# Hybrid decoder trunk: the gate projections of scan groups 1 to 3 as seven-product pairs ahead of the scan, and each scan interleaved with an output projection

## The reference

```python
def ssd_mixer(u, w_in, conv_w, conv_b, dt_bias, A_log, D, norm_w, w_out):
    proj = u @ w_in
    z = proj[..., :SSD_INNER]
    xbc = proj[..., SSD_INNER:SSD_INNER + SSD_CONV_DIM]
    ...
    xbc = jax.nn.silu(causal_depthwise_conv(xbc, conv_w, conv_b))
    ...
    y = ssd_chunked(xs, dt, A, Bm, Cm) + xs.astype(jnp.float32) * D.astype(jnp.float32)[:, None]
    y = y.reshape(b, s, SSD_INNER) * jax.nn.silu(z.astype(jnp.float32))
    yg = y.reshape(b, s, SSD_GROUPS, SSD_INNER // SSD_GROUPS)
    yg = yg * lax.rsqrt(jnp.mean(yg * yg, axis=-1, keepdims=True) + EPS)
    y = yg.reshape(b, s, SSD_INNER) * norm_w.astype(jnp.float32)
    return y.astype(u.dtype) @ w_out
```

## Time and profile before

| what | us |
|---|---|
| runs, median of 3 | 2283.34 (2282.04 to 2283.8) |
| profiled execution, its own time | 2282.14 |
| its span, first to last instruction | 2280.4 |
| PE busy in the span | 2258.5 |
| DVE busy | 1320.3 |
| POOL busy | 1320.6 |
| ACT busy | 1101.5 |

### The profile page before, as it was taken

How to read it: one execution, slowest core, us unless ns; L and a number is a source line. 1 busy time by engine, 2 the same in 40 slices (tenths; PEclk the granted TensorE clock), 3 DMA queues, 4 the chain that set the end, 5 groups by cost and what they waited for, 6 DMA issues and landing times.

```text
span 2280.4 us, 28960 instructions
## 1 busy us (share of the span) xinstructions
PE 2258.5 (99%) x10698; PEld 1845.5 (81%) x10698; DVE 1320.3 (58%) x1716; ACT 1101.5 (48%) x2016; POOL 1320.6 (58%) x950
## 2 busy tenths in 40 slices
PE   8999999999999999999999999999999999999998
PEld 6877888888888878888878888888888888888887
DVE  7357663333335798855568484747854343336777
ACT  4046544333333446655567474737643333334445
POOL 3224288777774664787734242334388777774654
PEclk9999999999999999999999999999999999999999
DMA  5100323323227855233263323232222323228744
GB/s 164 47 28 19 120 64 112 120 88 120 88 102 259 268 161 166 93 112 119 86 222 123 120 84 118 86 102 93 102 88 97 122 84 122 85 106 292 250 148 155
DMA packets 170807, 281.45 MB, mean 123 GB/s; under 512 B 19232, under 2 KB 104108, under 8 KB 168108
## 3 DMA queue, kind: packets, MB, share of 16 engines
q1 hardware_dynamic: 167084, 267.68, 34.9%
q10 hardware_dynamic: 3584, 11.93, 1.3%
HBM read 209.71 MB, written 69.86 MB: 123 GB/s over the span
## 4 chain that ended last, share of the span: by engine, by line
PE 92%; DVE 3%; POOL 2%; issue 1%; ACT 1%; DMA 1%; SPq 0%; ACTq 0%; DVEq 0%; POOLq 0%
PE ps L2212 44%; PE ps L1925 8%; PE ps L1927 8%; PE ps L1926 8%; PE ps L2302 5%; PE ps L2306 5%; PE ps L2298 5%; PE ps L2592 1%; PE ps L2582 1%; PE ps L2575 1%; PE ps L1948 1%; PE ps L2370 1%; POOL sq L1205 1%; PE ps L2135 1%; PE ps L2168 1%
## 5 line engine op out<-in xcount | busy, mean ns | idle before, releaser
L1051 POOL TENSOR_TENSOR s_lo<-s_val,s_hi 128x512 fp32r<-128x512 f32 x154 | 235.5, 1533 | 196.7 <-ACT s_hi L1575 196.0
L2862 DVE TENSOR_TENSOR xres<-ps,xres 128x512 f32<-128x512 f32 x132 | 90.5, 688 | 400.2 <-PE ps L2212 400.2
L947 POOL TENSOR_TENSOR w_lo<-w_raw,w_hi 128x1024 fp32r<-128x1024 f32 x50 | 119.3, 2387 | 270.6 <-ACT w_hi L1239 205.9
L972 POOL TENSOR_TENSOR p_lo<-p_val,p_hi 128x512 fp32r<-128x512 f32 x176 | 239.4, 1369 | 48.6 <-ACT p_hi L1380 37.5
L1380 ACT ACTIVATE p_hi<-p_val 128x512 fp32r<-128x512 f32 x176 | 111.0, 632 | 307.8 <-POOL p_val L998 307.8
L2212 PE MATMUL ps<-xn_hi,p_hi 128*128 128x512 f32 x704 | 189.0, 390 | 1.2 <-ACT xres L1483 1.2
L2212 PE MATMUL ps<-xn_lo,p_hi 128*128 128x512 f32 x704 | 188.2, 389 | 0.0
L2212 PE MATMUL ps<-xn_hi,p_lo 128*128 128x512 f32 x704 | 188.2, 389 | 0.0
L1575 ACT ACTIVATE s_hi<-s_val 128x512 fp32r<-128x512 f32 x154 | 97.0, 630 | 160.8 <-DMA d_val<-in_w_down 89.9
L1925 PE MATMUL ps<-xn_hi,w_hi 128*128 128x512 f32 x400 | 160.3, 401 | 0.0
L1926 PE MATMUL ps<-xn_lo,w_hi 128*128 128x512 f32 x400 | 156.0, 390 | 0.0
(11 more groups left out here) (361 smaller groups left out, 5570.3 us busy)
## 6 DMA issues: line engine op xcount, KB each, us to landing
s_val<-hidden SPq DMA_DIRECT2D x154, 256.0 KB, 2.9
hidden<-xres SPq DMA_DIRECT2D x20, 1792.0 KB, 6.5
wv_g<-in_w_gate SPq DMA_DIRECT2D x22, 1024.0 KB, 5.2
wv_u<-in_w_up SPq DMA_DIRECT2D x20, 1024.0 KB, 5.1
d_val<-in_w_down SPq DMA_DIRECT2D x70, 256.0 KB, 4.1
rows_v<-in_w_down SPq DMA_DIRECT2D x64, 256.0 KB, 3.8
mdec<-decay_sums SPq DMA_DIRECT2D x32, 512.0 KB, 4.2
xres<-parked_x SPq DMA_DIRECT2D x24, 512.0 KB, 6.0
```

The lines of the kernel that those rows point to most:

```text
L947: pool.tensor_tensor(w_lo[piece.slot][:, :], raw[piece.raw][:, :], f(w_hi[piece.slot][:, :]), ALU.subtract).then_inc(lo_done, 1)
L972: pool.tensor_tensor(p_lo[n][:, :, :], src, f(p_hi[n][:, :, :]), ALU.subtract).then_inc(p_lo_done, 1)
L1051: pool.tensor_tensor(s_lo[i][:, :], s_val[i][:, :], f(s_hi[i][:, :]), ALU.subtract)\
```

## The change

It has two halves. First, the gate columns of groups 1, 2 and 3 (six blocks of 256 columns) become blocks of the input stage: `NQ` goes from 6 to 9, and they are done with seven products each. ACT applies SiLU as it reads the finished row from PSUM; SP stores the row to a new DRAM tensor `z_rows` (12 rows of 512 KB) and loads it back in halves of 1 MB (`load_z`). Group 0's gates stay in its scan.

```diff
-        NQ = 6
+        NQ = 9
...
-        Q_BLOCKS = [(0, "x0"), (0, "x1")] + [(g, n) for g in range(1, G) for n in ("bc", "x0", "x1")]
+        Q_BLOCKS = ([(0, "x0"), (0, "x1")] + [(g, n) for g in range(1, G) for n in ("z0", "z1")]
+                    + [(g, n) for g in range(1, G) for n in ("bc", "x0", "x1")])
...
+                if is_z(i):
+                    sp.wait_ge(z_row_done, of_kind(i))
+                    sp.dma_start(z_rows[(g - 1) * BG + k - NCB], row_buffer(i)).then_inc(row_stored[i % 4], 16)
...
+            def load_z(g, half):
+                cols = slice(half * BANK, (half + 1) * BANK)
+                z_src = z_rows[(g - 1) * BG:g * BG].rearrange("r p s -> p r s")
+                sp.dma_start(zs_at, z_src[:, :, cols]).then_inc(z_loaded, 16)
...
+                if is_z(i):
+                    act.activation(row_buffer(i), flat(row_banks(i)), ACT.Silu).then_inc(z_row_done, 1)
+                    return
```

```diff
+        Z_ORDER = [(0, 0), (0, 1), (1, 0), (2, 0), (3, 0), (1, 1), (2, 1), (3, 1)]
+        Z_AFTER_CHUNK = [(5,), (6, 7), (8,), (9,), (10, 11), (12, 13), (14,), (15,)]
+        SILU_AFTER_CHUNK = {1: (0, 1), 3: (2, 3), 5: (4, 5), 7: (6,)}
...
+        def sums_after(g):
+            return {7: 0} if g == 0 else {3: 1, 6: 2} if g == 1 else {2: 2 * g - 1, 6: 2 * g}
...
+        PIECE_HI = [{0: 2, 1: 3, 3: 4, 4: 5, 5: 6, 6: 7}, {1: 0, 3: 1, 4: 2, 6: 3}, {0: 0, 2: 1, 4: 2, 6: 3}, {0: 0, 2: 1}]
...
+                if k:
+                    pe.wait_ge(cb_freed, k)
+                    pe.wait_ge(m_ready, 2 * k)
...
+                    if g == 0:
+                        for i in Z_AFTER_CHUNK[c]:
+                            z_half(i)
+                    else:
+                        for n in (2 * c, 2 * c + 1):
+                            out_part(g - 1, n, range(BG)).then_inc(out_full, 1)
+                    if c in sums_after(g):
+                        square_sums(sums_after(g)[c])
...
+            def between(g, c):
+
+                if g == 0:
+                    if c == 6:
+                        gated(0, 0)
+                    if c == 7:
+                        rests(0, 0, range(BG - 1))
+                    return
+                if c == 0:
+                    if g == 1:
+                        rest(0, 0, BG - 1)
+                    else:
+                        add_tile(g - 2, NT - 1)
+                        reciprocal_rms(2 * g - 2)
+                        gated(g - 1, 1)
+                elif (g, c) == (1, 1):
+                    reciprocal_rms(0)
+                elif (g, c) == (1, 5):
+                    reciprocal_rms(1)
+                elif g >= 2 and c == 4:
+                    reciprocal_rms(2 * g - 1)
+                if c:
+                    add_tile(g - 1, c - 1)
+                if (g, c) == (1, 1):
+                    gated(0, 1)
+                if c == 4:
+                    if g == 1:
+                        rests(0, 1)
+                    gated(g, 0)
+                if g >= 2 and c == 3:
+                    rests(g - 1, 1)
+                if c == 7:
+                    rests(g, 0)
...
-                        four = mdec[c % 2][:, 4 * hf:4 * hf + 4, :]
-                        dve.tensor_tensor(four, four, cbm[c % 2][:, :].unsqueeze(1).to_broadcast([P, 4, P]), ALU.mult)\
+                        dve.tensor_tensor(four, four, ps[:, CB, 0:P].unsqueeze(1).to_broadcast([P, 4, P]), ALU.mult)\
...
+                        dve.tensor_tensor(ps[:, YDIAG, :], ps[:, YDIAG, :], e2, ALU.add).then_inc(ydiag_summed, 1)
...
+                    if (g, c) == (1, 0):
+                        silu_z(ZU - 1)
+                        root(0)
+                    if (g, c) == (1, 2) or g >= 2 and c == 1:
+                        split(g - 1, 1)
+                    if (g, c) == (0, 6) or g and c == 5:
+                        split(g, 0)
+                    if c in PIECE_HI[g]:
+                        next_hi(g, PIECE_HI[g][c])
+                    if (g, c) == (1, 4):
+                        root(1)
+                    if g >= 2 and c == 3:
+                        root(2 * g - 1)
+                    if g and c == 7:
+                        root(2 * g)
```

803 lines of the change are left out of this document (467 added, 336 removed), and 3 rows, old and new, of the table LO_AHEAD.

## The result

The changed kernel takes **2294.51 us** (median of 5 runs, 2292.84 to 2295.47) against 2283.39 us for the kernel before (5 runs, 2282.04 to 2286.2): a ratio of 1.0045, 95% interval 1.0031 to 1.0060. It is 11.1 us slower. The forecast was 2276.5 us, a gain of 6.8 us, with a range of 2266 to 2289: the measured time has the other sign and lies outside the range.

The account below looks back on a forecast made before the run. PE's list of matmuls was taken as the bound. -16.3 - 1.6 + 4.6 + 1.6 + 2.9 + 2.0 = -6.8 us from the profiled 2282.1, median 1.2 higher: 2276.5 us, range 2266 to 2289.

Parts of the forecast that it names:

- Fewer matmuls, 16.3 us: Gate projection on PE, groups 1 to 3: 72 matmuls gone at 0.227 us each, 16.3 us less.
- Rival D: Longer input stage runs below PE's pace, rows passing through four buffers: 1 us per block, 2282.5 us; chance 0.06.
- The next term, 1.6 us: Ends of groups 0, 1 and 2: PE's three 0.52 us waits for POOL's sum of squares go, 1.6 us less.
- nothing too, as the loads are asked for a chunk and more ahead.: DMA: storing and reloading the 12 gate rows, 12 MB added to 281 MB, costs nothing.
- What the scan now hides: Scan: whether helpers' work fits each shortened chunk; a plain chunk fits with 2.2 us to spare on DVE.
- +4.6 us, group 0's chunk 7: Group 0's chunk 7: PE waits 4.6 us for `masked_decay`, late behind ACT's SiLU, squares, high parts and exponentials.
- +1.6 us at the border: Border of groups 0 and 1: ACT's SiLU, root and table loads cost 1.1 us for chunk 8, 0.5 for chunk 9.
- +2.9 us in group 1: Group 1: low parts and gatings share the fifth chunk on DVE, wait 2.7 us, with 0.2 more near chunk 2.
- +2.0 us in groups 2 and 3: Groups 2 and 3: DVE's low parts, then additions and gatings, cost waits of 0.3 and 0.7 us per group.
- rival C: Groups 1 to 3 DVE bound, gatings and low parts meeting POOL: 2297 us in full; chance 0.19.
- Rival E: DVE pays 0.04 us for each of 192 operations reading PSUM, half in waiting chunks: 2280.5 us; chance 0.05.
- Rival A: The forecast: saving real, 8 to 14 us given back, most in group 0 by ACT; 2271 to 2283 us; chance 0.47.

Follow-up runs that it names:

- Run 1: Changed kernel with SyncE asking for the fourth weight piece ahead of the gate and row loads in chunk 5 of groups 1 to 3: 2284.18 us.
- run 5: Changed kernel with group 0's weight pieces 4 and 5 asked for one chunk earlier: 2289.01 us.
- Run 11: Kernel before, with the masked product kept in PSUM and PE's wait for the mask moved to the chunk's start, nothing else: 2297.17 us.
- run 2: Changed kernel with the masked product of B and C back in SBUF and PE's early wait for the mask removed: 2281.07 us.
- run 6: Changed kernel with runs 1 and 2 together: 2275.99 us.
- run 3: Changed kernel with group 0's first-half squares and high parts behind chunk 7's exponentials on ACT, low parts in group 1's chunk 0: 2297.81 us.
- run 7: Run 3 with group 0's last weight piece also asked for ahead of group 1's rows: 2294.14 us.
- run 10: Changed kernel with runs 1, 2, 3, 5 and 7 together, three low parts moved a chunk earlier and the seventh SiLU moved beside the eighth: 2264.67 us.

## Why the prediction was wrong

**Fewer matmuls, 16.3 us.** Right. The input stage is gapless, and with the waits mended the kernel ends at 2264.67 us, where 2283.4 - 17.9 = 2265.5 was due. Rival D is out. The next term, 1.6 us, holds as well: the three square-sum waits are gone.

**"nothing too, as the loads are asked for a chunk and more ahead."** This step, the price of the added loads, failed first. I judged the DMA by its mean busy share (a third) and by the order in which the loads are asked for. I never asked what stands ahead of a weight piece in SyncE's queue, nor what stands behind its split on ACT, where the next exponentials do. Run 1 puts 10.3 us on the piece's place behind those loads in groups 1 to 3, run 5 puts 5.5 us on two pieces of group 0.

**"What the scan now hides", the chunk sums.** This is the second step that failed. I did let PE need the mask at the next chunk's start, but applied that only where I had added work to DVE. The mask ends at T + 7.02 in my own row, and the chunks that have one part of the gate projection (12 matmuls) on PE last 6.48 us: 0.5 us late by the new point already in the kernel before, without any addition. Group 0 has three such chunks. I summed chunks 6 to 9 there and took chunks 1 to 5 as free. Their waits came to 4.7 us, with 1.4 us of clock behind the longest (that one owes most of its length to a late piece: run 5 leaves 0.57 of its 3.36 us). Run 11 shows what the omission is worth by itself: 14.2 us. It and the late pieces overlap, as runs 1, 2 and 6 show (10.3, 13.4, together 18.5), since a late mask costs more the earlier PE asks for it.

**+4.6 us, group 0's chunk 7.** Measured 5.05 us of wait, ended by the mask, with the squares ahead of ACT's exponentials, as I had worked it out. So near a size is in part luck, for the cause was only half of it: the late weight piece behind the squares gave nearly the same wait alone (run 3, 4.70 us). The lost clock, 2.7 us, was not in the sum.

**+1.6 us at the border.** Too high: nothing in group 1's chunk 0 and 0.18 us in its chunk 1. PE had waited in chunk 7, which gave ACT and DVE time to catch up; when that wait went (run 7), one of 3.29 us stood at the border.

**+2.9 us in group 1.** The chunk with low parts and gatings gave 2.18 us against my 2.7, and chunk 2 gave 0.26 against 0.2. The 2.24 us in chunk 7 was unforeseen, and came from the piece.

**+2.0 us in groups 2 and 3.** Chunk 5 of group 2 gave 0.83 us against 0.7. Chunk 7 of group 2 gave 3.30 unforeseen, and group 3 gave nothing. In group 3 ACT splits no piece in the later chunks (`PIECE_HI` has chunks 0 and 2 only), so none stands ahead of chunk 7's exponentials, which fits. The period of group 2 came out as 81.2 us (1449.19 to 1530.38 on PE), which the list of signs gave to rival C; in run 10 it is 73.6 us, near the 74 worked out.

**Rival C** had nearly the right time, 2297, for a wrong reason. It had low parts and gatings on DVE lengthened by POOL. Few were: of 32 low parts the median fell from 1268 to under 750 ns, and the gatings kept theirs (680 and 686 ns) with a shorter longest one. The rows are the low parts of the first halves of groups 1 to 3 and the gatings of groups 1 to 3 in the changed kernel; shortest, median and longest in ns, beside the earlier trace rows:

```profile
L3554 DVE SCALAR_TENSOR_TENSOR y_lo_c<-rows_v,gconst,y_hi_c x12: 744/748/750, 1440.2 to 1598.0; 128x512 fp32r<-128x512 f32 x12
...
L3542 DVE TENSOR_TENSOR rows_v<-rows_v x24: 679/686/1790, 1409.6 to 1603.1; 128x512 f32<-128x512 f32 x24
```

**Rival E and the page's rule.** Neither the mask multiplication nor the y operation became longer by reading PSUM (1.28 against 1.29 us for two, 344 against 346 ns for one). The difference of fixed cost between SBUF and PSUM in the Trainium skill ("VectorE: DVE Perf Modes", the errata section) does not show in them.

**Rival A's words** do not fit its numbers: 8 to 14 us given back of 17.9 would be 2273 to 2279 us, and its range says 2271 to 2283. Neither holds the result; 29 us were given back.

The prediction did say which readings would refute its picture, a wait for DMA among them. It looked for that wait on PE, though, and it was two engines away, on ACT. What was missing from the list of rivals was a chain, DMA to ACT to DVE to PE, each link with slack of its own in the old profile.

## What to carry to other kernels

When a buffer goes and a wait moves earlier, list for every repetition how late the producer is against the new point; what was hidden lateness in the old trace becomes idle time, and it can be read off before the change is made. For each in-order queue, ask of every load what is ahead of it and what unrelated work stands behind its first user. A helper that holds up the bounding engine can have two sufficient causes, and then mending one alone shows nothing.
